# An encoder layer on one core: the attention's value product with both halves of the values in one stationary operand

## What is computed

```python
q = _rmsnorm(q.reshape(B, S, N_Q_HEADS, HEAD_DIM), q_norm_g)      # 8 heads of 64
k = _rmsnorm(k.reshape(B, S, N_KV_HEADS, HEAD_DIM), k_norm_g)     # 2 heads of 64
q, k = _apply_axial_rope(q, ...), _apply_axial_rope(k, ...)
s = jnp.einsum('bqkgd,bskd->bkgqs', qblk, k).astype(jnp.float32) * scale
p = jax.nn.softmax(s, axis=-1).astype(v.dtype)
o = jnp.einsum('bkgqs,bskd->bqkgd', p, v)
```

## Time and profile before

| | us |
|---|---|
| median of three runs | 1020.01 (1019.78 to 1020.21) |
| span of the profiled execution, first to last instruction | 1017.0 |
| around the span (median less span) | 3.0 |
| score of unit 0 starts | 203.14 |
| score of unit 63 starts | 310.80 |
| first late product of the output projection | 331.30 |

### The profile page before, as it was taken

How to read it: one execution, slowest core, us unless ns; L and a number is a source line. 1 busy time by engine, 2 the same in 40 slices (tenths; PEclk the granted TensorE clock), 3 DMA queues, 4 the chain that set the end, 5 groups by cost and what they waited for, 6 DMA issues and landing times.

```text
span 1017.0 us, 15253 instructions
## 1 busy us (share of the span) xinstructions
PE 981.6 (97%) x5074; PEld 827.6 (81%) x5074; DVE 829.5 (82%) x1092; ACT 745.9 (73%) x1001; POOL 161.3 (16%) x180
## 2 busy tenths in 40 slices
PE   8999999999999999949999999999999999999996
PEld 8997998877877888737888888888888888888884
DVE  6659898988885335677989998999999999989984
ACT  7447798487995346548878887888788888878873
POOL 1000000133793111130100110110011001100101
PEclk9999999999999999969999999999999999999998
DMA  7111101001102535379999999999999999999961
GB/s 267 48 42 30 38 28 43 1 1 63 63 1 80 212 108 204 116 283 412 409 391 392 391 411 392 392 390 412 392 392 395 407 392 392 404 398 392 382 189 21
DMA packets 75281, 248.45 MB, mean 244 GB/s; under 512 B 9388, under 2 KB 16616, under 8 KB 75240
## 3 DMA queue, kind: packets, MB, share of 16 engines
q1 hardware_dynamic: 70472, 231.12, 58.7%
q0 software_dynamic: 4752, 16.78, 6.5%
q10 hardware_dynamic: 16, 0.00, 0.0%
HBM read 231.11 MB, written 16.78 MB: 244 GB/s over the span
## 4 chain that ended last, share of the span: by engine, by line
PE 88%; DVE 5%; ACT 2%; POOL 2%; issue 1%; DMA 0%; DVEq 0%; POOLq 0%; ACTq 0%
PE bank L1050 26%; PE bank L1052 26%; PE bank L1051 26%; PE bank L1056 6%; PE bank L1215 1%; PE bank L1216 1%; POOL prob L645 1%; DVE e_lo L1829 1%; PE bank L1100 1%; PE bank L1248 0%; POOL wo_lo L637 0%; DMA xs<-h_rows,idx_all 0%; DVE xc L1576 0%; DVE row_stat L1636 0%; PE bank L1078 0%
## 5 line engine op out<-in xcount | busy, mean ns | idle before, releaser
L1050 PE MATMUL bank<-e_hi,xsT_hi 128*128 128x512 f32 x512 | 201.0, 393 | 1.2 <-DVE xsT_lo L1834 1.0
L1052 PE MATMUL bank<-e_hi,xsT_lo 128*128 128x512 f32 x512 | 199.3, 389 | 0.0
L1051 PE MATMUL bank<-e_lo,xsT_hi 128*128 128x512 f32 x512 | 199.3, 389 | 0.0
L975 ACT ACTIVATE e_hi<-raw_gate 128x1024 fp32r<-128x1024 f32 x128 | 134.7, 1061 | 33.3 <-PE bank L1052 31.7
L1829 DVE TENSOR_TENSOR e_lo<-raw_gate,e_hi 128x1024 fp32r<-128x1024 f32 x126 | 149.5, 1221 | 6.3 <-ACT e_hi L975 2.5
L1829 DVE TENSOR_TENSOR e_lo<-raw_down,e_hi 128x1024 fp32r<-128x1024 f32 x128 | 149.5, 1220 | 4.4 <-ACT e_hi L975 1.4
L1829 DVE TENSOR_TENSOR e_lo<-raw_up,e_hi 128x1024 fp32r<-128x1024 f32 x128 | 148.4, 1220 | 4.6 <-ACT e_hi L975 3.4
L975 ACT ACTIVATE e_hi<-raw_down 128x1024 fp32r<-128x1024 f32 x128 | 128.5, 1061 | 12.3 <-PE bank L1052 12.3
L975 ACT ACTIVATE e_hi<-raw_up 128x1024 fp32r<-128x1024 f32 x128 | 126.8, 1057 | 2.7 <-PE bank L1052 1.2
L1050 PEld LDWEIGHTS bank<-e_hi,xsT_hi 128*128 128x128 f32 x512 | 96.1, 188 | 21.5 <-DVE xsT_lo L1834 1.2
L1052 PEld LDWEIGHTS bank<-e_hi,xsT_lo 128*128 128x128 f32 x512 | 96.1, 188 | 20.0
(11 more groups left out here) (271 smaller groups left out, 2017.0 us busy)
## 6 DMA issues: line engine op xcount, KB each, us to landing
raw_gate<-in_exp_w_gate_dram SPq DMA_DIRECT2D x64, 1024.0 KB, 14.4
raw_up<-in_exp_w_up_dram SPq DMA_DIRECT2D x64, 1024.0 KB, 14.8
raw_down<-in_exp_w_down_dram SPq DMA_DIRECT2D x64, 1024.0 KB, 14.3
w_raw<-in_w_in_dram SPq DMA_DIRECT2D x6, 1024.0 KB, 5.3
wo_raw<-in_w_out_dram SPq DMA_DIRECT2D x8, 512.0 KB, 4.4
y_dram<-x SPq DMA_DIRECT2D x8, 512.0 KB, 5.1
h_rows<-h SPq DMA_DIRECT2D x8, 512.0 KB, 3.0
x_nat<-in_x_prompt_dram SPq DMA_DIRECT2D x4, 512.0 KB, 6.5
```

The costliest lines, as they stand in the source:

```text
L975: act.activation(e_hi[:, (8 * m + j) % SPLIT, :], raw[:, j // 2, j % 2, :], ACT.Copy).then_inc(row_hi, inc)
L1050: pe.matmul(out, l_hi, r_hi, start=first, stop=False)
L1051: pe.matmul(out, l_hi, r_lo, start=False, stop=False)
L1052: return pe.matmul(out, l_lo, r_hi, start=False, stop=last)
```

## The change

- `v_hi` and `v_lo` become one tensor `v_parts`: for each key block and k/v head three pieces of 64 columns, high, low, high. A stationary operand of 128 columns is then high and low (even heads) or low and high (odd heads). A unit's value product is two matmuls, with the high and with the low half of the probabilities. Each head has a bank of its own, with 64 rows from the high values and 64 from the low ones.
- After each head (not each pair) ScalarE copies the 64 rows of the low values to the other half's partitions (`low_half`), VectorE adds them to the rows of the high values (`mixA`, now in SBUF). After the second head of a pair, one slot later, ScalarE copies `mixA` to `mixA_hi`, and `mixA_lo` is the difference, on GpSimd for the first three pairs and behind the reciprocal on VectorE for the others.
- The first seven heads use bank 6, with the first product of a head put off by a slot and a wait for the head before; later heads alternate between banks 6 and 7.
- VectorE takes reciprocals two at a time in even slots, for units n - 2 and n - 1.
- Token blocks 4 to 7 of q and k are split on GpSimd in four instructions, behind slots 4, 8, 12 and 20.
- The zero columns and their clearings go; the third piece is copied by GpSimd. Some semaphores are merged.

```diff
-    VW = (2 * KVH + 1) * HD
-    v_hi = [at(f"v_hi{s}", R1 + o * K, [P, BPS, VW], F32R) for s, o in enumerate((80, 90))]
-    v_lo = [at(f"v_lo{s}", R1 + o * K, [P, BPS, VW], F32R) for s, o in enumerate((97, 85))]
+    v_parts = [at(f"v_parts{s}", R1 + (80 + 6 * s) * K, [P, BPS, KVH, 3, HD], F32R) for s in range(SEQS)]
+    low_half = at("low_half", R1 + 92 * K, [P, S], F32)
+    mixA = at("mixA", R1 + 94 * K, [P, S], F32)
...
-    beside = {3: [("hi", 4)], 4: [("lo", 4)], 8: [("hi", 5)], 9: [("lo", 5)], 13: [("hi", 6)], 14: [("lo", 6)],
-              16: [("v", 1)], 19: [("hi", 7)], 20: [("lo", 7)]}
+    beside = {4: [("pair", 4)], 8: [("pair", 5)], 12: [("pair", 6)], 16: [("v", 1)], 20: [("pair", 7)]}
...
+    HEADS_ONE_BANK = 7
+    POOL_PAIRS = 3
+
+    def out_bank(head):
+
+        return 6 if head < HEADS_ONE_BANK or head % 2 == 0 else 7
+
+    def late_head(v):
+
+        return v % BPS == 0 and 0 < v // BPS < HEADS_ONE_BANK
...
-        sp.wait_ge(qk_lo_done, NB)
+        sp.wait_ge(qk_lo_done, 3 * BPS)
...
+        def split_pair(b):
+
+            qp, kp = q_pair[pair_set(b)], k_pair[pair_set(b)]
+            pool.wait_ge(qk_norm_done, UNITS_QK)
+            if b >= BPS + 2:
+                pool.wait_ge(qkT_done, last_turn(b - 2) + 1)
+            q_in, k_in = q_heads(b), k_heads(b).unsqueeze(2).to_broadcast([P, KVH, 2, HD])
+            q_hi = qp[:, :, 0, :].rearrange("p (g h) d -> p g h d", g=2)
+            pool.tensor_copy(q_hi.bitcast(F32R), q_in).then_inc(qk_hi_done, 1)
+            pool.tensor_copy(kp[:, :, 0, :, :].bitcast(F32R), k_in).then_inc(qk_hi_done, 1)
+            pool.wait_ge(qk_hi_done, BPS + 2 * (b - BPS) + 1)
+            pool.tensor_tensor(qp[:, :, 1, :].rearrange("p (g h) d -> p g h d", g=2).bitcast(F32R), q_in, q_hi, ALU.subtract).then_inc(qk_lo_done, 1)
+            pool.wait_ge(qk_hi_done, BPS + 2 * (b - BPS) + 2)
+            pool.tensor_tensor(kp[:, :, 1, :, :].bitcast(F32R), k_in, kp[:, :, 0, :, :], ALU.subtract).then_inc(qk_lo_done, 1)
...
                 pool.tensor_scalar(prob[:, u % PROB_SLOTS, :], prob[:, u % PROB_SLOTS, :], row_stat[:, 2, u:u + 1], 1.0,
                                    ALU.mult, ALU.mult).then_inc(prob_done, 1)
+                pair = last_of_pair(n - V_LAG - 2)
+                if pair is not None and pair < POOL_PAIRS:
+                    pool.wait_ge(mixA_hi_done, pair + 1)
+                    pool.tensor_tensor(mixA_lo[mix_of(pair)], mixA[:, :], mixA_hi[mix_of(pair)].bitcast(F32), ALU.subtract).then_inc(mixA_lo_done, 1)
...
                 u, t, v = n, n - T_LAG, n - V_LAG - 1
-                if v >= 0 and v % (2 * BPS) == 2 * BPS - 1:
-                    pair = v // (2 * BPS)
-                    head = 2 * pair
+                head, pair = last_of_head(v), last_of_pair(v - 1)
+                if head is not None:
                     act.wait_ge(pv_done, v + 1)
-                    act.activation(mixA_hi[:, head % HQ // 2, head // HQ * S:(head // HQ + 1) * S], bank[:, out_bank(pair), :],
-                                   ACT.Copy).then_inc(mixA_hi_done, 1)
+                    if head >= 2:
+                        act.wait_ge(head_summed, head - 1)
+                    act.activation(low_half[value_rows(head), :], bank[other_rows(head), out_bank(head), :], ACT.Copy).then_inc(low_half_done, 1)
+                if pair is not None:
+                    act.wait_ge(head_summed, 2 * pair + 2)
+                    act.activation(mixA_hi[mix_of(pair)], mixA[:, :], ACT.Copy).then_inc(mixA_hi_done, 1)
...
-            product(bank[:, out_bank(pair), :], v_hi[s][:, kc, cols], v_lo[s][:, kc, cols], probT_hi[:, kc, :], probT_lo[:, kc, :],
-                    head % 2 == 0 and kc == 0, head % 2 == 1 and kc == BPS - 1).then_inc(pv_done, 1)
+            both_parts = v_parts[s][:, kc, g, odd:odd + 2, :].rearrange("p a d -> p (a d)")
+            out = bank[:, out_bank(head), :]
+            pe.matmul(out, both_parts, probT_hi[:, kc, :], start=(kc == 0), stop=False)
+            pe.matmul(out, both_parts, probT_lo[:, kc, :], start=False, stop=(kc == BPS - 1)).then_inc(pv_done, 1)
...
-                if v >= 0 and v % (2 * BPS) == 2 * BPS - 1:
-                    pair = v // (2 * BPS)
-                    head = 2 * pair
+                head, pair = last_of_head(v), last_of_pair(v - 1)
+                if head is not None:
+                    if head % 2 == 0 and head:
+                        dve.wait_ge(mixA_lo_done, head // 2)
+                    dve.wait_ge(low_half_done, head + 1)
+                    rows = value_rows(head)
+                    dve.tensor_tensor(mixA[rows, :], bank[rows, out_bank(head), :], low_half[rows, :], ALU.add).then_inc(head_summed, 1)
+                if 0 < u <= UNITS and u % 2 == 0:
+                    dve.wait_ge(exp_done, u)
+                    dve.reciprocal(row_stat[:, 2, u - 2:u], row_stat[:, 1, u - 2:u]).then_inc(recip_done, 2)
+                if pair is not None and pair >= POOL_PAIRS:
                     dve.wait_ge(mixA_hi_done, pair + 1)
-                    where = (slice(None), head % HQ // 2, slice(head // HQ * S, (head // HQ + 1) * S))
-                    dve.tensor_tensor(mixA_lo[where], bank[:, out_bank(pair), :], mixA_hi[where].bitcast(F32), ALU.subtract).then_inc(mixA_lo_done, 1)
-                if 0 <= u - 1 < UNITS:
-                    dve.wait_ge(exp_done, u)
-                    dve.reciprocal(row_stat[:, 2, u - 1:u], row_stat[:, 1, u - 1:u]).then_inc(recip_done, 1)
+                    dve.tensor_tensor(mixA_lo[mix_of(pair)], mixA[:, :], mixA_hi[mix_of(pair)].bitcast(F32), ALU.subtract).then_inc(mixA_lo_done, 1)
```

89 lines of the change are left out of this document (41 added, 48 removed).

## The result

The changed kernel takes 1038.32 us (median of four runs, 1037.60 to 1038.93), the kernel before 1020.11 us in the runs beside it: a ratio of 1.0179, 95% interval 1.0167 to 1.0192. That is slower, as forecast, but by 18.2 us where the forecast said 3.6, and outside the range.

A forecast was written before the change was run, and what follows sets the result against it. The prediction took TensorE to bound the kernel, waiting for T(4h) behind GpSimd after the change. Start +2.0, steps 1 to 6 -4.2, steps 7 to 14 +5.2 and tail +0.6 gave +3.6: 1023.6 us, range 1013.5 to 1028.5.

The forecast's parts named there:

- T(4h): Transposes of a head's first key block, released by GpSimd's scaling; TensorE was to wait 0.57 us per head for it.
- The start: S(0) to S(7), starts of scores 0 and 7: splitting q and k on GpSimd delays block 4's transposes, +2.0 us.
- GpSimd's part of the chain: Between reciprocal and T(4h): a second scaling adds 0.66 us and, in five steps, a split between the scalings 1.27.
- rival (b): GpSimd's splits run before the reciprocal, T(4h) staying near 5.1 in steps 8 to 13: 1014.4 us; chance 0.20.
- (c): The product is all that counts, TensorE at 1.37 us a slot throughout: 1008.6 us; chance 0.05.
- T(4h) "at S + 4.49": Transposes 4.49 us after S, the score start of unit 4h+3, read from the last head; a second scaling made it 5.15.
- steps 7 to 14: S(31) to S(63), four slots a step: GpSimd's and ScalarE's splits delay T(4h), 58.4 against 53.2 us, +5.2.
- The clock: Rival: VectorE's order costs more, or waits lower TensorE's clock, 1.7 us each time: 1027 to 1030 us; chance 0.15.
- Steps 1 to 6: S(7) to S(31), with late transposes and fewer value matmuls: 41.7 against 45.9 us, -4.2.
- six waits for bank 6: New heads 1 to 6: the sum is there at S + 3.5, TensorE arrives at 3.6, so nothing extra.
- rival (e): VectorE's subtractions with two SBUF operands and GpSimd's reads exclude each other: at most 5.1 us, 1028.7 us; chance 0.05.
- The tail: S(63) to the late output product: T(60) 0.66 later, copy and addition 1.3, value products save 1.4; sum +0.6 us.

The follow-up runs named there:

- fifth experiment: Changed kernel with token blocks 4 to 7 of q and k split again by ScalarE and VectorE: 1040.06 us.
- eighth experiment: Changed kernel with GpSimd's five subtractions that stood behind a slot 4h+3 moved one slot later: 1030.55 us.
- eleventh experiment: Changed kernel with a third matmul per value product again, the low half of the probabilities used twice: 1038.01 us.
- fourth experiment: Changed kernel with 18 unread transposes of the identity on TensorE ahead of its wait for T(4h) of six heads: 1032.18 us.
- twelfth: The ninth with additions and `mixA_lo` back ahead of `probT_lo`: 1020.30 us, 0.9991 to 1.0010 of the kernel before.
- fourteenth to sixteenth experiments: Twelfth with ScalarE's low-row copies shortened from head 8, 1016.36 us; eight more ScalarE copies in the kernel before, 1022.49, and in the twelfth, 1025.82.
- first experiment: Changed kernel with reciprocals taken one by one, still behind the head's addition: 1025.94 us.
- third: Changed kernel with reciprocals taken one by one and ahead of the head's addition: 1023.30 us.
- seventeenth: The twelfth with the low rows of heads 9, 11, 13 and 15 copied by VectorE instead of ScalarE: 1020.16 us.
- ninth: The third with splits spread thinner, block 4 split before slot 0, additions and `mixA_lo` behind `probT_lo` from head 7: 1023.27 us.

## Why the prediction was wrong, point by point

**What held.** Slower, through T(4h) waiting for GpSimd. The start: +2.0 forecast, +2.1 measured, with GpSimd's four instructions at 210.65 to about 213.5 where the forecast had 3.1 us for them; the fifth experiment shows the cause, 2.04 us. GpSimd's part of the chain: from the reciprocal to T(4h) it was priced at 0.24 + 0.66 + 1.27 + 0.75 = 2.9 us, and step 8 has 270.32 to 273.21, 2.9. GpSimd's splits between the two scalings are real (eighth experiment), and rival (b), that they find room, fell: T(32) stands at S + 8.06 and T(36) at S + 7.98, not near 5.1. That the product is all that counts (c) fell most clearly (eleventh experiment).

**The step that failed: T(4h) "at S + 4.49", the reciprocal 0.99 us ahead of it, for every head.** The sum puts the reciprocal of unit 4h + 3 at S + 3.50 in each of steps 7 to 14, plus ScalarE's splits of that slot: 30.5 us for the eight together. In the changed kernel it stands at S + 4.39 to 5.17, 38.1 us together. These 7.5 us are most of the 9.0 by which the steps exceed their 58.4; the exclusion in steps 9 and 13 adds 0.9, and the slow matmuls behind T(4h) 1.2 (S(39) comes 1.44 us behind T(32) and S(55) 1.63 behind T(48), where 0.96 was forecast). With the filler of the fourth experiment the same eight reciprocals stand at 35.4 us together: so 2.7 of the 7.5 come by the lower clock, and 4.9 are there at nearly the full one.

The S + 3.50 was read from slots 63 and 64, where no splits are left and ScalarE has slack: the exponential of unit 63 starts at S + 1.59. In steps 7 to 14 of the changed kernel those of units 4h + 3 start at S + 1.69 to 2.44. The trace of the kernel before already showed this. Here is its step 9, with no split of ScalarE in slot 39; those of slots 37 and 38 are enough to put the exponential at S + 2.34 and the reciprocal at S + 4.30:

```profile
270.38 0.39 PE L1215 MATMUL bank<-kT,qT 128*128 128x512 f32 x1
...
272.72 0.70 ACT L896 ACTIVATE prob<-bank,row_stat 128x512 f32<-128x512 f32 x1
...
273.38 0.62 ACT L881 ACTIVATE mixA_hi<-bank 128x512 fp32r<-128x512 f32 x1
...
274.68 0.15 DVE L1645 RECIPROCAL row_stat<-row_stat 128x1 f32<-128x1 f32 x1
```

So the prediction took ScalarE as latency (the splits that stand in front of a copy) and not as load. The earlier trace rows had it busy 50.45 of 53.21 us in this very piece, and the change adds eight copies of 0.59 us: 50.45 + 4.7 = 55.2 us, before a single wait. This is what a mended order meets: the twelfth and the fourteenth to sixteenth experiments stand 1.9 to 2.6 us above ScalarE's busy time. It is not what sets the changed kernel's 67.45, for 55.2 lies below the forecast's own 58.4, and ScalarE idles 10.4 us there. That its load is what makes the exponentials late in the changed kernel itself is argued from these runs; no run took its copies away there.

In the terms of the sum: with reciprocals one by one the prediction's steps would have been 58.4 - 8 x 0.66 - 5 x 1.27 = 46.8 us; the first experiment has 58.94. That is 12 us too low. The pairs, priced at the remaining 11.6 us, measure 67.45 - 58.94 = 8.5. The two errors partly cancel, and 9.0 us are left of the 58.4.

**The clock.** It stood among the rivals, "at 1.7 us each time", with 0.15, and not in the sum. The waits of 3.34, 2.14, 3.21 and 2.34 us in steps 8, 9, 12 and 13 were each followed by matmuls at 1.2 GHz, those of 1.22 and 1.83 us in steps 10 and 11 were not: the granted clock of the eight steps is 1.00, 0.94, 0.87, 0.80, 1.00, 0.92, 0.88 and 0.78. The length of the wait does not settle it alone, since the eleventh experiment has one of 2.21 us in step 8 and a clock of 1.00 in step 9. The fourth experiment puts the clock at about 6 us in all. The forecast waits were 1.8 us and more in five steps (5.15 + 1.27 against 4.58), and the earlier trace rows had shown the clock at 0.62 after an idle TensorE: the row was there, and it belonged in the forecast and not in a rival, because the forecast itself said that TensorE would idle.

**Steps 1 to 6.** -4.2 forecast, -2.1 measured. Step 1 took 8.04 where 7.6 was forecast, steps 2 to 6 35.7 where 34.1 was. That the six waits for bank 6 cost nothing extra was wrong: of the 2.8 us for which TensorE waits for the addition, 1.7 us in four waits of up to 0.94 lie here (the fifth, 1.1 us, is in step 7), and with quicker steps it is more (3.0 us in five in the twelfth). The kernel before waits 1.4 us in two places for `mixA_lo` there, so this is a small part of the miss. The granted clock of this piece is 0.95, where it was 0.97, and this is a part of it too; how much was not measured by itself.

**The exclusion, rival (e).** It came in full in two places, with 0.44 us at each between the reciprocal and T(4h), and is worth about 2 us with the clock behind it, not 5.1. The place named for it was right; that the reciprocal stands ahead of `mixA_lo` gave no shelter, since the scaling behind GpSimd's split is hit as well.

**The tail.** +0.6 forecast, +2.7 measured. T(60) comes at 331.52, S + 5.95 and not 5.15, as ScalarE and VectorE are late there too, and the clock of the piece is 0.93. The last 2.6 us, behind the late product, were forecast at nothing. 1.5 of them lie before the first residual addition of the output (3.09 us behind the late product before, 4.63 after). The wait in front of the late product is 2.64 us where it was 1.65, and behind it the clock is at its lower level, where it was at the full one; the first 3.5 us behind the late product, before and after, columns as in the earlier trace rows:

```profile
331.30:334.80 3.50, 3.50 (x15) 2.88 (x16) 1.55 (x3) 1.21 (x2) 0.00 (x0) 1.00 1.00 404
```

```profile
348.76:352.26 3.50, 3.50 (x9) 2.78 (x10) 1.15 (x2) 1.59 (x3) 0.00 (x0) 0.52 1.01 411
```

Fewer matmuls fit into the same time. The remaining 1.1 us I can't place. The profiled executions differ by 1.9 us more than the medians.

**What stays open.** Step 10 of the ninth and twelfth experiments takes over 8 us. By their traces VectorE's `mixA_lo` holds `probT_lo` back by 0.7 us, and two of GpSimd's splits then stand ahead of two scalings; neither was taken away by itself.

## What to carry to other kernels

Before an edit moves work off the busiest engine, add what it puts on the second busiest to that engine's busy time in the same piece: if that sum is longer than the piece, the gain is gone, and the sum is the least that the piece can take. Waits come on top of it: 55.2 us here, 56.0 to 57.3 in the three orders that wait least (the third, twelfth and seventeenth experiments), and 67.45 in the changed kernel. And a chain of waits must be read where the engines are as loaded as in the piece that is forecast, not in its last head. Small instructions at the head of a release chain (a reciprocal of 0.15 us) were not worth batching here: what they release waits for the last of the batch, and other work of the released engine gets in between. Where a forecast contains an idle TensorE of about 2 us or more, as five steps of this one did, the lower clock behind it belongs into the sum.

## What the runs showed of the hardware

- Behind waits of TensorE of 2.1 to 3.3 us within a busy stage its granted clock fell to 0.78 to 0.94 over the step, in matmuls of 0.63 and 0.78 us instead of 0.39 and 0.47; idle transposes in these waits gave 6.1 us back.
- A copy or addition over 64 partitions takes as long as one over 128: 0.59 us on ScalarE (0.60 in the earlier trace rows) and 0.68 on VectorE (0.69 there).
- GpSimd's cast of 128x512 to the shorter form is cheaper than forecast, 0.56 us from start to start, and its half-width one 0.36; a subtraction is 1.23.
- VectorE's 128x512 subtraction with both operands in SBUF takes 1.18 us when it starts under a GpSimd subtraction, and a GpSimd scaling that starts under it takes 1.14 instead of 0.69.
